# One core of Trainium2, a hybrid decoder: the long convolution's TensorE share between attention heads, its norms under the output projection

## The reference

```python
z = h @ w_in                                  # conv_in (2048), q_lat, kv_lat, k_rope
u = a * sigmoid(g)                            # 1024 channels
u = causal_depthwise_conv(u, conv_w, conv_b)  # 31 taps
u = silu(layernorm(u, conv_ln_g, conv_ln_b))
# q, k from the latents, rotated; 8 heads, causal softmax
attn = causal_attention(q_full, k_full, v)    # 1024 channels
mix = concat([rmsnorm(u, conv_out_norm), rmsnorm(attn, attn_out_norm)]) @ w_out
x = x + rmsnorm(mix, post_mix_norm)
hf = rmsnorm(x, pre_ffn_norm)                 # then a gated feed-forward
```

## Time and profile before

| | |
|---|---|
| median of 3 runs | 2650.33 us (2645.78 to 2650.72) |
| the profiled execution | 2641.45 us, span 2639.7 us |
| TensorE busy | 2523.8 us, 96% of the span |
| VectorE busy | 1664.9 us, 63% |
| ScalarE busy | 1273.9 us, 48% |
| chain that ended last | TensorE 88%, VectorE 8%, ScalarE 2% |
| mean granted clock of TensorE | 0.977 |

### The profile page before, as it was taken

How to read it: one execution, slowest core, us unless ns; L and a number is a source line. 1 busy time by engine, 2 the same in 40 slices (tenths; PEclk the granted TensorE clock), 3 DMA queues, 4 the chain that set the end, 5 groups by cost and what they waited for, 6 DMA issues and landing times.

```text
span 2639.7 us, 37271 instructions
## 1 busy us (share of the span) xinstructions
PE 2523.8 (96%) x14610; PEld 2197.2 (83%) x14610; DVE 1664.9 (63%) x2176; ACT 1273.9 (48%) x1633; POOL 62.7 (2%) x57
## 2 busy tenths in 40 slices
PE   8989698999999999998999999998999999999997
PEld 7878387888888888887889989886788888888886
DVE  6899566665656554447766346866767667675454
ACT  5455455544444443445453334754554544444342
POOL 0000000000000000000003210000000000000000
PEclk9999699999999999999999999999999999999998
DMA  7553044565555554653653234554455556555553
GB/s 239 174 144 112 0 160 144 176 190 184 185 188 190 191 191 155 212 184 107 212 168 101 92 120 162 174 179 140 143 188 184 188 189 191 191 188 186 181 186 120
DMA packets 236031, 436.22 MB, mean 165 GB/s; under 512 B 14408, under 2 KB 32856, under 8 KB 235792
## 3 DMA queue, kind: packets, MB, share of 16 engines
q1 hardware_dynamic: 232384, 423.66, 49.8%
q0 software_dynamic: 2240, 6.80, 0.8%
q10 hardware_dynamic: 1296, 4.19, 0.4%
HBM read 432.51 MB, written 3.69 MB: 165 GB/s over the span
## 4 chain that ended last, share of the span: by engine, by line
PE 88%; DVE 8%; ACT 2%; issue 1%; DMA 1%; DVEq 0%; SPq 0%; ACTq 0%
PE ps L754 48%; PE ps L757 24%; DVE w_lo L439 2%; PE ps L763 2%; PE ps L765 2%; PE ps L766 2%; DVE ar L1168 2%; PE ps L1192 1%; PE ps L1411 1%; PE ps L2018 1%; PE ps L2024 1%; PE ps L740 1%; PE ps L743 1%; PE ps L742 1%; PE ps L1235 1%
## 5 line engine op out<-in xcount | busy, mean ns | idle before, releaser
L439 DVE TENSOR_TENSOR w_lo<-w_raw,w_hi 128x1024 fp32r<-128x1024 f32 (+3 forms) x820 | 993.6, 1217 | 771.0 <-ACT w_hi L433 769.7
L754 PE MATMUL ps<-x,w_hi 128*128 128x512 f32 x4320 | 1370.9, 399 | 45.4 <-issue 20.4
L433 ACT ACTIVATE w_hi<-w_raw 128x1024 fp32r<-128x1024 f32 (+3 forms) x820 | 853.1, 1045 | 934.0 <-PE ps L757 841.6
L757 PEld LDWEIGHTS ps<-x,w_lo 128*128 128x128 f32 x4320 | 818.4, 189 | 194.4
L757 PE MATMUL ps<-x,w_lo 128*128 128x256 f32 x4320 | 854.1, 279 | 0.0
L754 PEld LDWEIGHTS ps<-x,w_hi 128*128 128x128 f32 x4320 | 665.1, 190 | 49.3 <-issue 37.1
L754 PE MATMUL ps<-h,w_hi 128*128 128x512 f32 x1408 | 444.1, 397 | 4.4 <-DVE w_lo L439 4.4
L757 PEld LDWEIGHTS ps<-h,w_lo 128*128 128x128 f32 x1408 | 265.2, 188 | 62.8
L757 PE MATMUL ps<-h,w_lo 128*128 128x256 f32 x1408 | 277.1, 278 | 0.0
L754 PEld LDWEIGHTS ps<-h,w_hi 128*128 128x128 f32 x1408 | 215.1, 189 | 5.1 <-DVE w_lo L439 5.0
L475 ACT ACTIVATE half<-ps 128x512 f32<-128x512 f32 x170 | 99.4, 592 | 101.2 <-PE ps L757 101.2
(11 more groups left out here) (306 smaller groups left out, 1727.1 us busy)
## 6 DMA issues: line engine op xcount, KB each, us to landing
w_raw<-in_w_gate SPq DMA_DIRECT2D x88, 1024.0 KB, 5.1
w_raw<-in_w_up SPq DMA_DIRECT2D x88, 1024.0 KB, 5.1
w_raw<-in_w_down SPq DMA_DIRECT2D x88, 1024.0 KB, 5.1
w_raw<-in_w_in SPq DMA_DIRECT2D x79, 1024.0 KB, 5.1
w_raw<-in_w_out SPq DMA_DIRECT2D x32, 1024.0 KB, 5.1
w_raw<-in_w_xkv SPq DMA_DIRECT2D x8, 1024.0 KB, 5.0
w_raw<-in_w_uq SPq DMA_DIRECT2D x18, 256.0 KB, 3.7
w_raw<-in_w_ukv SPq DMA_DIRECT2D x16, 256.0 KB, 3.9
```

Source lines behind the costliest of these rows:

```text
L433: nc.scalar.activation(w_hi[:, u % HIS, 0:ks.stop - ks.start, cs], w_raw[:, slot(g, j), ks, cs], ACT.Copy)\
L439: nc.vector.tensor_tensor(w_lo[:, slot(g, j), ks, cs], w_raw[:, slot(g, j), ks, cs], w_hi[:, u % HIS, 0:ks.stop - ks.start, cs].bitcast(F3 ...
L754: nc.tensor.matmul(bank, w_h(k, cs), x(k).rearrange("p a n -> p (a n)"), start=(n == 0 and k == 0), stop=False)
L757: ins = nc.tensor.matmul(bank[:, T:2 * T], w_l(k, cs), x(k)[:, 0, :], start=False, stop=(final and k == ks.stop - 1))
```

## The change

- `diag_steps` writes the diagonals as ScalarE's filler in uq and ukv, six a step, into parts of x2 and of `ar` that are free by then; chunk 7 first, then chunk 6.
- `long_conv_pe` becomes a generator. Three steps (12 taps of chunk 7) run before the rotation, five (19 taps) behind it; chunk 6 goes in 16 steps of two taps, two ahead of head 0 and two in each head until they are done. Its outputs lie in banks 2 and 3.
- VectorE's 24 remaining tap steps, which ran between rotation and attention, go three behind each head (`attention_rest_dve`). The folding of attention's first four squares goes behind head 6.
- The mean's folds follow attention (`conv_sums_dve`); mean and attention's squares are summed by TensorE in one go, one half of bank 7 each.
- w_out becomes one turn in the narrow form, its groups ordered by row halves: attention's rows for column groups 0 to 2 ("part": left in PSUM), the convolution's rows for them ("sum"), then all rows for group 3. All eight banks are used.
- The norms of the convolution (`conv_norms_*`) become the filler of w_out on all three engines; layernorm's scaling and Silu in halves of four chunks; ln is summed ahead of unit 4, conv ahead of unit 9.
- `mix_evict`: squares and gained copies are taken by ScalarE straight from PSUM, two outputs at a time.

```diff
-            Gemm("w_out", 2, [group(w_loop(A["w_out"], 0 + b * P, 2 * W), 4, out=(ar, M1 + b, 8), kind="sum")
-                        for b in (0, 4)], x2c),
+            Gemm("w_out", 1, [group(attn_first(w_cols(A["w_out"], W * c, W), p0), tiles, out=(ar, M1 + 4 * c, 0), kind=kind, p0=p0, banks=2 * c)
+                              for p0, tiles, kind, cs in ((0, 2, "part", (0, 1, 2)), (8, 2, "sum", (0, 1, 2)), (0, 4, "sum", (3,)))
+                              for c in cs],
+                 lambda p: x2c((p + 8) % DC), form="narrow"),
...
+        def mix_evict(act, g, i, gr):
...
+            for b in range(2):
+                c, n, _, bank = pair(gr, b)
+                group_ready(act, g, i, gr, b)
+                ins = nc.scalar.activation(sq_buf[q % 2][:, c:c + n, :], bank, ACT.Square)
...
+                for m in range(c, c + n):
+                    nc.scalar.activation(where[:, base_c + m, :], bank[:, m - c, :], ACT.Copy,
+                                         scale=col("post_mix", 4 * q + m)).then_inc(geared, 1)
...
+        def diag_steps(act):
+
+            act.wait_ge(products, AHEAD_P + G["uq"].p0)
             act.wait_ge(aux_loaded, 16 * N_AUX)
-            for c in range(CV, CC):
+            for k, c in enumerate((CC - 1, CV)):
                 for s in range(CONV_K):
...
+                    if s % 6 == 5:
+                        yield
...
+            pe.wait_ge(evicted, G["ukv"].e0 + 2)
+            for k, c in enumerate((CC - 1, CV)):
                 for s in range(CONV_K):
...
+                    if s % (4, 2)[k] == (3, 1)[k] or s == CONV_K - 1:
+                        yield
...
             attn_scores(pe, a, 0)
             attn_scores(pe, a, 1)
+            if filler:
+                next(filler)
+                next(filler)
             for h in range(a.heads):
                 attn_turn(pe, a, h)
                 if h + 2 < a.heads:
                     attn_scores(pe, a, h + 2)
+                if filler:
+                    next(filler, None)
                 attn_weigh(pe, a, h)
...
         def conv_norms_pe(pe):
...
+            yield from idle(3)
             sum_pe(pe, "ln")
...
+            yield from idle(5)
             sum_pe(pe, "conv")
...
+        def attention_rest_dve(dve, taps):
+
+            for h in range(H):
+                for _ in range(3):
+                    next(taps, None)
+                if h == 6:
+                    reduce_dve(dve, "attn", 0, 4)
+                yield
...
+            filler = diag_steps(act)
+            run_("uq", filler, stat=["q", "kv"])
             ahead_("ukv")
-            run_("ukv")
+            run_("ukv", filler)
...
+            conv_sums_dve(dve)
             reduce_dve(dve, "attn", 1, 4)
-            prep_dve(dve, "conv", u_src, gain_of("conv_out"))
             refine(dve, "attn")
-            apply(dve, attn_src, H)
+            apply(dve, attn_src, 2)
+            apply(dve, attn_src, 6, 2)
             prep_dve(dve, "attn", attn_src, gain_of("attn_out"))
-            run_("w_out")
+            filler = conv_norms_dve(dve)
+            next(filler)
+            run_("w_out", filler)
...
+            conv = long_conv_pe(pe)
+            for _ in range(3):
+                next(conv)
             rope_pe(pe)
-            long_conv_pe(pe)
+            for _ in range(5):
+                next(conv)
...
+            finish(conv)
+            pe.wait_ge(summed, STATS["mean"][1] + STATS["mean"][2])
+            sum_pe(pe, "attn", "mean")
+            multiply(pe, G["w_out"], filler=conv_norms_pe(pe))
```

More of the change, by code:

```diff
@@ L466, in evict_act @@
             M = len(gr["at"])
+            if g.name == "w_out":
+                if gr["kind"] == "sum":
+                    mix_evict(act, g, i, gr)
+                return
             if gr["form"] == "wide":
@@ L718, in body @@
                     if filler and u:
-                        next(filler)
+                        next(filler, None)
                     gr, j, ks, _ = unit(g, u)
                     n, jj = u - 2 * gr["t"], j - gr["t"]
-                    final = n == 2 * gr["tiles"] - 1
+                    final = n == 2 * gr["tiles"] - 1 and gr["kind"] != "part"
                     pe.wait_ge(lo_done, g.u0 + u + 1 + i * g.units)
-                    pe.wait_ge(*g.needs(jj * gr["kc"] + ks.stop))
+                    pe.wait_ge(*g.needs(gr["p0"] + jj * gr["kc"] + ks.stop))
+                    if g.name == "w_out" and gr["kind"] == "part" and gr["banks"] == 2 and n == 0:
+                        pe.wait_ge(tap1, CV * CONV_K + CC - CV)
                     if n == 0:
@@ L733, in body @@
                     w_l = lambda k, c: w_lo[:, slot(g, j), k, c]
-                    x = lambda k: g.x(jj * gr["kc"] + k)
+                    x = lambda k: g.x(gr["p0"] + jj * gr["kc"] + k)
+                    first = n == 0 and not (g.name == "w_out" and gr["p0"])
                     if gr["form"] == "swap":
@@ L763, in body @@
                                 nc.tensor.matmul(out_m, w_h(k, cs), x(k)[:, 0, :],
-                                                 start=(n == 0 and k == 0 and m % 2 == 0), stop=False)
+                                                 start=(first and k == 0 and m % 2 == 0), stop=False)
                                 nc.tensor.matmul(out_m, w_h(k, cs), x(k)[:, 1, :], start=False, stop=False)
@@ L806, in build @@
         STATS = {}
-        for name, parts in [("x", 4), ("q", 2), ("kv", 1), ("mean", 2), ("ln", 2), ("conv", 2), ("attn", 2),
+        for name, parts in [("x", 4), ("q", 2), ("kv", 1), ("attn", 2), ("mean", 2), ("ln", 2), ("conv", 2),
                             ("mix", 4), ("ffn", 4), ("ff", 4), ("mix2", 4), ("mem", 4), ("xq", 4),
@@ L812, in build @@
         PREPS = {}
-        for name, n, first in [("x", 16, 0), ("q", 6, 0), ("kv", 4, 6), ("conv", 8, 0), ("attn", 8, 8),
+        for name, n, first in [("x", 16, 0), ("q", 6, 0), ("kv", 4, 6), ("attn", 8, 8), ("conv", 8, 0),
                                ("ffn", 16, 0), ("mix2", 16, 0), ("gdn", 8, 0), ("moba", 8, 8), ("mem", 16, 0),
@@ L2103, in conv_norms_act @@
         def conv_norms_act(act):
-            root(act, "mean")
-            yield
             for k in range(2):
@@ L2118, in conv_norms_act, with mean_folds @@
                 square_act(act, "conv", k, u_src, 4, lambda c: (ln_out, c + 1))
-            yield
+            yield from idle(2)
             root(act, "conv")
             yield
-            square_act(act, "attn", 0, attn_src, 4, lambda c: (o_kept, c + 1))
+            act.wait_ge(conv_pe, 2)
+            prep_act(act, "conv", u_src, gain_of("conv_out"), lambda c: (applied, 5 if c < 2 else 6))
             yield
-        def conv_norms_dve(dve):
-            dve.wait_ge(conv_pe, 1)
+        def mean_folds(dve):
+            for k in range(2):
+                y = span(u_src, 4 * k, 4)
+                v = half[:, 2 * k:2 * k + 2, :]
+                dve_chain.link(dve, nc.vector.tensor_tensor(v, y[:, 0:2, :], y[:, 2:4, :], ALU.add))
+                nc.vector.tensor_tensor(ssq[:, 2 + k, :], v[:, 0, :], v[:, 1, :], ALU.add).then_inc(summed, 1)
@@ L2128, in conv_norms_dve, with conv_sums_dve @@
+        def conv_sums_dve(dve):
+            dve.wait_ge(conv_pe, 2)
             for c in range(CV, CC):
-                nc.vector.tensor_scalar(ar[:, Z1 + c, :], ps[:, c - CV, 0:T], col("conv_b", c), None, ALU.add)\
+                nc.vector.tensor_scalar(ar[:, Z1 + c, :], ps[:, 2 + c - CV, 0:T], col("conv_b", c), None, ALU.add)\
                     .then_inc(tap1, 1)
             dve.wait_ge(tap1, CV * CONV_K + CC - CV)
-            for k in range(2):
-                reduce_dve(dve, "mean", k, 4, u_src)
@@ L2145, in conv_norms_dve @@
             yield
-            apply(dve, u_src, CC)
+            for k in range(2):
+                apply(dve, u_src, 4, 4 * k)
+                yield
             yield
```

135 lines of the change are left out of this document (82 added, 53 removed).

## The result

The changed kernel ran in 2621.47 us (median of 4 runs, 2617.7 to 2622.0), the kernel before beside it in 2648.06: ratio 0.9905, 95% interval 0.9886 to 0.9924. Its profiled execution took 2621.72 us around a span of 2619.9, against 2641.45 and 2639.7 before: the two traces differ by 19.8 us, and the sum had said 16.4.

What follows compares the result with a forecast made beforehand. TensorE bounds the kernel, except for a hole in attention made by the convolution's norms between heads. 0.8 - 16.7 - 12.3 + 13.8 - 2.0 = -16.4 us, taken from the 2650.3 median: 2634, range 2623 to 2644.

Steps and rivals of the forecast that it cites:

- the sum: Whole profiled execution: the five stage terms added together, -16.4 us, which would read 2625.
- The level: Last step: the runs' median, 2650.3, stands 8.9 us above the profiled execution; gain taken from the median, giving 2634.
- Stage 1: uq and ukv, where the diagonals move as filler: +0.8 us, bounds 0 and +3.
- Stage 2: End of ukv to first score: taps fill the wait, rotation at full clock; -16.7 us, bounds -17 and -14.5.
- Stage 3: First score to the projection's first product: heads of 5.0 us, then a longer tail; -12.3 us, bounds -16 and -7.
- Stage 4: The projection, with the norm chain as filler: stalls, sums, narrow form and slow start; +13.8 us, bounds +5 and +21.
- Stage 5: Projection's last product into the next stage: ScalarE squares straight from PSUM; -2.0 us, bounds -3 and -1.
- A: Projection: the norm chain fits under it, stalls of 9.5 us vanish but for the sums; 2625 us, chance 0.11.
- C: Projection: stalls double, or unit 12 onward waits for a chain never catching up; +10, 2644 us, chance 0.08.
- B: Attention: heads come slower than 5.0 us; at 6.0 a head +7 over seven heads, 2641 us, chance 0.12.
- D: Projection: three stops keep TensorE at 1.2 GHz, 2.8 us more per unit; twelve units give 2666; chance 0.05.
- E: Table loads for the Silu and next stage cost 1.4 us more each; +2.8, 2637 us, chance 0.04.

Runs made afterwards that it cites:

- a1: The changed kernel run again, nothing edited; 2625.11 us, ratio 0.9922 to the kernel before.
- a2: The changed kernel run once more as yardstick, nothing edited; 2622.38 us, ratio 0.9907 to the kernel before.
- e_front: Changed kernel with chunk 6's 31 taps all run ahead of attention, none between the heads; 2646.24 us, ratio 1.0007 to the kernel before.
- e_nonorm: Changed kernel without the convolution's norms under the projection, its raw sums scaled, split and multiplied instead; ratio 0.9890 to the kernel before.
- e_fill: Kernel before with early diagonals and 12 taps ahead of the rotation, the other 50 behind it but ahead of attention; ratio 0.9998.
- e_bwarm: Kernel before, nothing moved, plus 8 products of 128 columns in each head whose result nobody reads; 2651.3 us, ratio 1.0028.
- e_dose: e_front plus 32 passes between heads whose result nobody reads, two in each half head; 2633.09 us, ratio 0.9964 to the kernel before.

## Why the prediction was right or wrong

**The level, wrong, 8.9 us.** The step that failed is the last one: "the median of the runs, 2650.3, stands 8.9 above it, and I take the gain from the median". Of that kernel, medians of 10 to 29 runs were 2643.2 to 2646.1, and that of the 29 was 2644.4. So 5.9 of the 8.9 us are a median of three that lay high, and 3.0 are a first profiled execution that lay low. The difference was read as a property of the kernel where it was spread. Of the 12.5 us of error, 8.9 are this and 3.4 the sum; 0.2 is rounding. Either of them put right alone would have left the time inside the range. The trace's own time less 16.4, 2625, was in the text, but that it comes nearer is partly luck: from 2644.4 the sum gives 2628, and the 16 runs of after, a1 and a2 have their median at 2622.5.

**Stage 1, +0.8: measured +1.0. Stage 2, -16.7: measured -16.8.** The first score came at 247.17; in three traces of each kernel it moves by up to 0.9 us, so agreement to 0.2 is closer than the traces can tell. The rotation ran at full clock, 1.89 us for 8 passes (3.60 before).

**Stage 3, -12.3: measured -15.6.** The term that was mis-sized is the head: 5.0 forecast, 4.7 measured, TensorE full as said. I added the lengths of bars, and a group's bar runs past the start of the next group (the turn's 0.49 us from 258.29, with the scores beginning at 258.62); start to start the same passes take 0.33, 1.98, 0.94, 0.65 and 0.84 us, 4.74 together. First score to turn 7 was 38.7 us for 41.3, and the tail 16.6 for 17.3, with its parts nearly as forecast (the sums begin 6.5 us after turn 7 for 6.9, 4.29 of it idle; at slow clock they take 3.78 for 4.0).

More than the size, the reason was incomplete. The sum took 4.53 us as what an undisturbed head needs and 3.4 us of TensorE's work in it, both from a head at full clock, and added 1.6 for eight passes to get 5.0. In that kernel sums of squares lay between the heads; take the norms away and put nothing in, and a head is not 4.5 but 6.43 (e_front). That it was those sums which kept the clock up in the earlier trace rows is argued, not shown. The eight passes were priced as a cost and are what keeps each head 1.7 us shorter. The sum came near since the passes were there, which for the clock is luck: for e_front the same reasoning said 10 to 12 us above the changed kernel, and ffn's first product came 21.4 later, about 10 us off.

**Stage 4, +13.8: measured +13.5.** The steps hold one by one. Stop before the convolution's sum 28.9 us after the first product forecast, work up to it ended at 28.9 (331.33); 2.57 idle for 3.6; the sum at slow clock 1.90 for 2.0; stop at unit 12 1.79 for 2.2; none at unit 8, where 0.5 was said. Slow start 2.0 for 1.5. The narrow form is confirmed by e_nonorm: projection and what follows within 0.3 us of the price. There the rule named in the prediction, "TensorE: Matmul & The Clock Gate", Back-to-back issue gap, of the Trainium skill, would have had the products of 256 columns 0.109 us apart, which the page gives for a product by itself; this trace has 0.120, and the row was the one to use.

**Stage 5, -2.0: measured -2.4.** Variance at 411.12 us, 3.5 after the last product (3.9 forecast).

**The rivals.** A fell (the stops are there), and so did C. B fell in sign: heads came faster than 5.0. D fell in the projection (clock 0.95; slow for 4.4 us at its start and for about 3.5 us behind each of two stops), but its mechanism is what decides between the heads, where it was not looked for. E fell: no time appeared behind the table loads (the one for the Silus ends at 321.52, and what the Silus at 322.13 wait for is VectorE).

**Slips in the working**, each worth at most 0.2 us of the forecast: the tail's terms add up to 17.1, not 17.3, and stage 5's to 3.7, not 3.9; twelve slow units are 33.6 us, not 32; and beside the convolution's products ran ScalarE's diagonals too.

**Which part earned it.** e_fill (the gap filled, all taps still ahead of attention) gains nothing; e_front (everything but the convolution between heads) gains nothing; e_bwarm (only a busier TensorE) loses 7 us. Together they give 20 in the first two traces, and somewhat more over all of them: ffn's first product stands at 438.1, 438.7 and 439.9 in three traces of the kernel before and at 417.8, 416.8 and 417.2 in three of the changed one, 21.6 us by the means. The ratios, 0.9905, 0.9922 and 0.9907, say 21 to 25 us; the 2 us beyond the traces' stage sums are within the spread shown above and are not explained further.

## What to carry to other kernels

A loop that waits a little in every turn was seen here at either of TensorE's clocks (0.50 us of wait a head at 1.2 GHz, 0.39 at 2.4): before moving work out from between its steps, ask what will hold the clock up there, and before pricing a step from a row, look at the granted clock of that row and at what stood beside it. Fill a stop before the clock has fallen and only where the stop outlasts the filling. Make the sum against the profiled execution's own time, and don't carry the result over to a median of few runs without knowing the kernel's spread.

## What the runs showed of the hardware

Two paces of one loop: the same heads took 6.43 us each with TensorE busy 92% of the time at clock 0.50 (e_front, six heads without change), and 4.52 with half of the extra passes, busy 91% at 1.00 (e_dose). In e_front the clock fell in a stop of 2.16 us before turn 0 and did not return until the projection, 5 us behind its first product; in the changed kernel eight passes (1.98 us) fill that stop, 0.24 is left of it, and the clock stays. The Trainium skill, "TensorE: Matmul & The Clock Gate", A second HAM failure mode: psum-queue depth-cycling, tells of short idle stretches between groups of products that make the clock swing. e_front shows short stops too (0.50 us a head), but its clock doesn't swing, it stays down.

The same instructions of the third attention took 19.5 to 22.9 us, and the mixer 570.6 or 573.7, from one execution to another: 3 us each, as much as an edit one would like to judge. Both go with the granted clock: over the third attention it was 0.91 where that took 19.5 or 19.6 us and 0.68 to 0.71 where it took 22.0 to 22.9.
